# A norm by token halves, summed in PSUM and turned on TensorE, between an attention block and the last feed-forward layer

## What is computed

```
for i in range(DEPTH_2):                       # i = 1 is the last layer
    mix = ... moba_attention(h, b_w_qkv, b_w_out)   # ends in o @ w_out, 1024x1024
    h = layer_norm_2(DEEPNORM_ALPHA * h + mix, ln1_g[i], ln1_b[i])
    h = layer_norm_2(DEEPNORM_ALPHA * h + swiglu(h, f_w13[i], f_w2[i]), ln2_g[i], ln2_b[i])

def swiglu(x, w13, w2):
    g, u = jnp.split(x @ w13, 2, axis=-1)
    return (jax.nn.silu(g) * u) @ w2
```

## Time and profile before

| what | value |
|---|---|
| median of 3 runs | 1174.18 us |
| the profiled execution | 1169.08 us, its span 1167.3 us |
| PE busy, whole span | 1109.0 us, 95% |
| DVE, ACT busy | 807.5 us (69%), 614.9 us (53%) |
| mean granted TensorE clock | 0.986 |
| attention ends, output projection | about 924 to 957 us |
| norm x5 | 957 to 971 us |
| last feed-forward net | 971 to 1159 us |

### The profile page before, as it was taken

One profiled execution on the slowest core, in us unless ns is written; L12 is line 12 of the kernel. 1 busy time (PEld: TensorE's weight loads), 2 busy tenths in 40 slices (PEclk: granted clock), 3 DMA queues, 4 the chain that ended last, 5 costly groups with the idle time before them and its releaser, 6 DMA issues.

```text
span 1167.3 us, 20553 instructions
## 1 busy us (share of the span) xinstructions
PE 1109.0 (95%) x8544; PEld 1068.4 (92%) x8544; DVE 807.5 (69%) x1360; ACT 614.9 (53%) x1028; POOL 3.3 (0%) x13
## 2 busy tenths in 40 slices
PE   7998989999999998879989999999999999999997
PEld 7998878899999987679989999999999799999996
DVE  7988489877878787586666755555589656555555
ACT  5567444555555648742454554545455545545453
POOL 0000000000000000000000000000000000000000
PEclk9999999999999998989989999999999999999998
DMA  9985247257666523234224266565536332665620
GB/s 377 418 314 179 74 145 279 95 175 246 229 223 210 180 76 113 61 102 146 73 73 143 70 205 198 183 197 184 160 120 201 130 128 91 217 198 181 197 75 37
DMA packets 58557, 195.60 MB, mean 168 GB/s; under 512 B 10848, under 2 KB 11232, under 8 KB 58208
## 3 DMA queue, kind: packets, MB, share of 16 engines
q1 hardware_dynamic: 58464, 194.28, 49.1%
HBM read 192.94 MB, written 1.31 MB: 166 GB/s over the span
## 4 chain that ended last, share of the span: by engine, by line
PE 73%; DVE 17%; ACT 7%; issue 2%; SPq 1%; DMA 0%; POOL 0%; ACTq 0%; DVEq 0%; POOLq 0%
PE ps L512 61%; DVE lo L1475 4%; PE ps L725 3%; ACT hi L1008 2%; DVE raw L1462 2%; PE ps L610 2%; PE ps L519 2%; DVE B L1484 1%; PE ps L531 1%; DVE ev L1713 1%; DVE st L1492 1%; PE ps L507 1%; DVE ev L1710 1%; DVE B L1788 1%; DVE B L1497 1%
## 5 line engine op out<-in xcount | busy, mean ns | idle before, releaser
L512 PE MATMUL ps<-hh,hi 128*128 128x256 f32 x1792 | 511.2, 285 | 15.2 <-DVE hl L1509 3.5
L512 PE MATMUL ps<-hh,lo 128*128 128x256 f32 x1792 | 504.3, 281 | 0.0
L512 PE MATMUL ps<-hl,hi 128*128 128x256 f32 x1792 | 503.9, 281 | 0.0
L1475 DVE TENSOR_TENSOR lo<-raw,hi 128x1024 fp32r<-128x1024 f32 x311 | 378.2, 1222 | 171.9 <-ACT hi L1008 171.1
L512 PEld LDWEIGHTS ps<-hh,hi 128*128 128x128 f32 x1792 | 340.7, 190 | 19.9 <-issue 9.6
L1008 ACT ACTIVATE hi<-raw 128x1024 fp32r<-128x1024 f32 x311 | 324.2, 1051 | 51.9 <-PE ps L512 51.6
L512 PEld LDWEIGHTS ps<-hl,hi 128*128 128x128 f32 x1792 | 340.6, 190 | 1.1
L512 PEld LDWEIGHTS ps<-hh,lo 128*128 128x128 f32 x1792 | 340.7, 190 | 0.0
L512 PE MATMUL ps<-fh,hi 128*128 128x256 f32 x392 | 109.9, 280 | 3.9 <-ACT B L1112 2.9
L512 PE MATMUL ps<-fh,lo 128*128 128x256 f32 x392 | 108.8, 278 | 0.0
L512 PE MATMUL ps<-fl,hi 128*128 128x256 f32 x392 | 108.8, 277 | 0.0
(11 more groups left out here) (256 smaller groups left out, 1221.8 us busy)
## 6 DMA issues: line engine op xcount, KB each, us to landing
raw<-in_w SPq DMA_DIRECT2D x359, 512.0 KB, 4.2
B<-in_t SPq DMA_DIRECT2D x2, 512.0 KB, 4.8
xa<-in_x SPq DMA_DIRECT2D x1, 1024.0 KB, 10.4
B<-in_r SPq DMA_DIRECT2D x1, 1024.0 KB, 6.0
out<-h SPq DMA_DIRECT2D x4, 256.0 KB, 2.0
cst<-in_c SPq DMA_DIRECT2D x1, 864.0 KB, 8.3
B<-between SPq DMA_DIRECT2D x32, 4.0 KB, 1.6
vec<-in_v SPq DMA_DIRECT2D x1, 328.5 KB, 6.7
```

The costliest lines, as they stand in the source:

```text
L512: m = g.matmul(o, l, r, start=first and n == 0, stop=last and n == 2, skip_group_check=True)
L1475: g.tensor_tensor(lo[:, j % SPLIT, :], raw[:, PLACE[j] % RAW, :], hi[:, j % SPLIT, :].bitcast(F), ALU.subtract).then_inc(*up("lo", j))
```

## The change

It moves the residual and the norm between attention and the last net from channel-major to token-major, and takes the first four pairs of the last net in another cut.

- The old state (x4) is carried into banks 0 to 3 by `carry_in` before the projection; `bout` uses `rows_out_of`, so that the sum of residual and projection stands in PSUM by tokens: banks 0, 1 for tokens 0 to 127, banks 2, 3 for tokens 128 to 255. The last three units finish the first token half, then the second.
- `norm_tokens` takes statistics straight from PSUM, normalises a token half into `nt` (left 512 channels on DVE, right 512 on ACT), PE turns it (`turn_tok`, 8 transposes a half), and gain, bias and split follow in 128x128 pieces (`affine`, `high_part`, `low_part`; the right four channel chunks together in one 128x512 split). The residual add, both sums over channels and the 52 constant matmuls are gone.
- The weights of the first four pairs come as eight units `w13r1` by rows (128 channels x [512 gate | 512 up]) in place of eight tiles; `absorb` multiplies them into banks 0 to 3 by token halves: chunks 0 to 3 of the first half, with the second half's turn after the third, chunks 0 to 3 of the second half, then chunks 4 to 7 of both. Gate, product, eight transposes and one split on 128x512 per half give the four chunks for w2.

```diff
+def downs_at(j):
+    return {4: (0, 1), 5: (2, 3), FF - 1: ()}.get(j, (j - 2,))
...
+PARTS = ((0, 1), (1, 2), (2, 3), (3, 4), (4, 8))
...
-    w += swiglu(1)
+    w += [("w13r1", k) for k in range(8)]
+    for j in range(4, FF):
+        w += [("w131", j), ("w131", FF + j)] + [("w21", d) for d in downs_at(j)]
+    w += [("w21", FF - 3), ("w21", FF - 2), ("w21", FF - 1)]
...
+            def turn_tok(nid, c, frees):
+                for half in range(2):
+                    s.wait_ge(*at("norm_a" if half else "norm_v", (nid, c)))
+                    s.wait_ge(*frees[half])
+                    for i in range(4):
+                        k = 4 * half + i
+                        m = g.transpose(bank[4 + 2 * c + half][:, i * P:i * P + P], nt[:, c, k * P:k * P + P], ident)
+                    m.then_inc(*up("turned", (nid, c, half)))
+            def absorb(kind, nid, frees):
+                turn_tok(nid, 0, frees[0])
+                def unit(k, c):
+                    j = UNIT[kind, k]
+                    wh, wl = slot(j)
+                    v = slice(c * P, c * P + P)
+                    s.wait_ge(*at("lo", j))
+                    s.wait_ge(*at("hl", (nid, part_of(k), c)))
+                    for n in range(2):
+                        m = three(bank[2 * c + n][:, :], wh[:, n * 512:n * 512 + 512], wl[:, n * 512:n * 512 + 512],
+                                  hh[:, k, v], hl[:, k, v], k == 0, k == 7, flip=True)
+                    if c:
+                        m.then_inc(*up("unit", j))
+                for k in range(4):
+                    unit(k, 0)
+                    if k == 2:
+                        turn_tok(nid, 1, frees[1])
+                for k in range(4):
+                    unit(k, 1)
+                for k in range(4, 8):
+                    unit(k, 0)
+                    unit(k, 1)
+            def ffn_tokens(kup, kdown, kr, nid, frees):
+                def down(j, cs):
+                    rows_out_of(kdown, j, fh[:, j % 4, :], fl[:, j % 4, :], at("f4_lo", (kup, 1)) if j < 4 else at("f_lo", (kup, j)),
+                                cs, j == FF - 1)
+                absorb(kr, nid, frees)
+                for j in range(4, FF):
+                    for half in (0, 1):
+                        t = 2 * j + half
+                        tile(kup, j + half * FF, R3[t % 4], nid, at("ff_out", (kup, t - 4)) if t > 11 else
+                             at("f4_lo", (kup, t - 10)) if t > 9 else at("n_a" if half else "n_v", (nid, 7 if half else 3, 0)))
+                        if t == 8:
+                            for c in range(2):
+                                s.wait_ge(*at("f4", (kup, c)))
+                                s.wait_ge(*at("n_v", (nid, 3, 1)))
+                                s.wait_ge(*at("n_a", (nid, 7, 1)))
+                                for i in range(4):
+                                    m = g.transpose(bank[6 + c][:, i * P:i * P + P], half_ev[:, c, i * P:i * P + P], ident)
+                                m.then_inc(*up("f4_mm", (kup, c)))
+                    if j == 4:
+                        for k in range(8):
+                            carry_in(nid, k)
+                    for d in downs_at(j):
+                        down(d, (0, 1))
+                for c in range(2):
+                    for j in (FF - 3, FF - 2, FF - 1):
+                        down(j, (c,))
...
+            def bout(k, cs):
+                rows_out_of("bout", k, hh[:, k, :], hl[:, k, :], at("att_lo", k), cs, k == 7)
             turned(0)
             turned(1)
+            s.wait_ge(*at("v_a", 1))
+            s.wait_ge(*at("v_v", 3))
+            for k in range(4):
+                carry_in("x4", k)
             apply(0)
             turned(2)
+            for k in range(4, 8):
+                carry_in("x4", k)
             apply(1)
-            for k in range(8):
-                rows_in("bout", k, 0, hh[:, k, :], hl[:, k, :], at("att_lo", k), k == 0, k == 7,
-                        [at("v_a", 1), at("v_v", 3)] if k == 0 else [])
+            for k in range(5):
+                bout(k, (0, 1))
                 if k < 5:
                     turned(k + 3)
                 if k < 6:
                     apply(k + 2)
-            after("x5", lambda k: at("res", ("x5", k - k % 2)))
-            ffn("w131", "w21", "x5", at("hl", ("x5", 0)), tokens=True)
+            bout(5, (0,))
+            apply(7)
+            bout(6, (0,))
+            bout(7, (0,))
+            for k in range(5, 8):
+                bout(k, (1,))
+            ffn_tokens("w131", "w21", "w13r1", "x5", [[at(*a_free[4 + 2 * c + half]) for half in range(2)] for c in range(2)])
...
+            def norm_tokens(nid, gain, bias, j):
+                def deviation(c):
+                    s.wait_ge(*at("tmv", (nid, c)))
+                    g.activation(frs[:, c, :], fmv[:, c, 1:2], ACT.Sqrt, bias=eps[:, 0:1]).then_inc(*up("tsd", (nid, c)))
+                def normed(c):
+                    s.wait_ge(*at("tnm", (nid, c)))
+                    g.activation(nt[:, c, 512:1024], bank[2 * c + 1][:, :], ACT.Identity, scale=frs[:, c, :],
+                                 bias=fnm[:, c, :]).then_inc(*up("norm_a", (nid, c)))
+                def affine(c):
+                    s.wait_ge(*at("turned", (nid, c, 1)))
+                    for k in range(4, 8):
+                        i = (k - 4) * P
+                        g.activation(xa[:, k, c * P:c * P + P], bank[5 + 2 * c][:, i:i + P], ACT.Identity, scale=gain(k),
+                                     bias=bias(k)).then_inc(*up("n_a", (nid, k, c)))
+                def high_part(c, p):
+                    a, b = PARTS[p]
+                    s.wait_ge(*at("n_v" if a < 4 else "n_a", (nid, b - 1, c)))
+                    g.activation(hh[:, a:b, c * P:c * P + P], xa[:, a:b, c * P:c * P + P], ACT.Copy).then_inc(*up("hh", (nid, p, c)))
+                deviation(0)
+                high(j)
+                normed(0)
+                high(j + 1)
+                high_part(0, 0)
+                high_part(0, 1)
+                deviation(1)
+                high_part(0, 2)
+                normed(1)
+                high_part(0, 3)
+                affine(0)
+                for p in range(4):
+                    high_part(1, p)
+                high_part(0, 4)
+                affine(1)
+                high_part(1, 4)
...
+            def norm_tokens(nid, kind, gain, bias, j):
+                def stats(c):
+                    s.wait_ge(*(at("unit", UNIT[kind]) if c else at("tok", kind[0])))
+                    for n in range(2):
+                        g.bn_stats(fst[:, c, 6 * n:6 * n + 6], bank[2 * c + n][:, :]).then_inc(*up("tbn", (nid, c, n)))
+                    s.wait_ge(*at("tbn", (nid, c, 1)))
+                    g.bn_aggr(fmv[:, c, :], fst[:, c, :].rearrange("p (i n) -> p i n", i=2)).then_inc(*up("tmv", (nid, c)))
+                def normed(c):
+                    s.wait_ge(*at("tsd", (nid, c)))
+                    g.reciprocal(frs[:, c, :], frs[:, c, :]).then_inc(*up("trs", (nid, c)))
+                    s.wait_ge(*at("trs", (nid, c)))
+                    g.scalar_tensor_tensor(out=fnm[:, c, :], in0=fmv[:, c, 0:1], scalar=-1.0, in1=frs[:, c, :], op0=ALU.mult,
+                                           op1=ALU.mult).then_inc(*up("tnm", (nid, c)))
+                    g.tensor_scalar(nt[:, c, 0:512], bank[2 * c][:, :], fmv[:, c, 0:1], frs[:, c, :], ALU.subtract,
+                                    ALU.mult).then_inc(*up("norm_v", (nid, c)))
+                def affine(c, k):
+                    s.wait_ge(*at("turned", (nid, c, 0)))
+                    g.tensor_scalar(xa[:, k, c * P:c * P + P], bank[4 + 2 * c][:, k * P:k * P + P], gain(k), bias(k), ALU.mult,
+                                    ALU.add).then_inc(*up("n_v", (nid, k, c)))
+                def low_part(c, p):
+                    a, b = PARTS[p]
+                    v = slice(c * P, c * P + P)
+                    s.wait_ge(*at("hh", (nid, p, c)))
+                    g.tensor_tensor(hl[:, a:b, v], xa[:, a:b, v], hh[:, a:b, v].bitcast(F),
+                                    ALU.subtract).then_inc(*up("hl", (nid, p, c)))
+                stats(0)
+                normed(0)
+                low(j)
+                affine(0, 0)
+                affine(0, 1)
+                low_part(0, 0)
+                low_part(0, 1)
+                stats(1)
+                affine(0, 2)
+                low_part(0, 2)
+                normed(1)
+                affine(0, 3)
+                low(j + 1)
+                low_part(0, 3)
+                affine(1, 0)
+                affine(1, 1)
+                low_part(1, 0)
+                low_part(1, 1)
+                affine(1, 2)
+                affine(1, 3)
+                low_part(1, 2)
+                low_part(1, 3)
+                low_part(0, 4)
+                low_part(1, 4)
```

(42 more changed lines are left out.)

50 lines of the change are left out of this document (40 added, 10 removed).

## The result

| | median, us | runs | lowest to highest |
|---|---|---|---|
| before | 1172.61 | 15 | 1167.59 to 1174.87 |
| after | 1164.13 | 15 | 1160.44 to 1170.11 |

The ratio is 0.9933, with an interval of 0.9917 to 0.9949: faster, as forecast. Two later comparisons of the same two kernels gave 0.9961 [0.9946, 0.9976] and 0.9948 [0.9928, 0.9967], 5.2 and 7.1 us between the medians where this one has 8.5.

What follows compares the result with a forecast made beforehand. PE bounds the last net, so the 13.84 us hole ahead of it is the prize; less 3.1 carry, 1.65 turn and pause, 0.87 second turn, 0.87 pairs, 0.4 to 0.5 waits: gain 6.9 us, forecast 1167.3 us, range 1165.0 to 1171.5.

Steps and rivals of the forecast that it cites:

- The sum: Whole kernel: eight tiles' end moves from 993.4 to 986.5, gain 6.9 us; taken off 1174.18 this gives 1167.3.
- The carry of the old state: Sixteen products ahead of the projection cost 3.57 us, 0.43 covered, so the projection starts 3.14 us late.
- The projection by tokens: Attention's output projection: 12 matmuls of 512 columns per unit, 2.80 us; nothing won or lost, end at 960.20.
- The norm of the first half: Under the projection's last three units, 4.2 us: row ready before PE ends; without them 3.7 us would stand open.
- Turn and first unit: Between projection and last net: transposes 0.87 us, affine and splits, first matmul at 961.85; PE pauses 0.8 us.
- Eight units by token halves: Start of the last net: 96 matmuls 22.4 us, second turn 0.87, waits 0.5; all end at 985.6.
- What follows: Behind the eight units: four pairs' transposes add 0.87 us; gates and products are hidden, x5's carry stays 3.57.
- The fallen clock: Rival at the turn ahead of the last net: pause grows to about 2.9 us, time 1171.1; chance 0.07.
- The converters don't bind: Denies the rival that ACT and DVE bind the alternating halves: gain about 0, 1174; chance 0.06, half near 1170.
- the net gives nothing back: Denies the rival that weights bind the last net, earlier start becoming later wait: 1174.2, no change; chance 0.03.
- no low clock runs through the units: Denies the rival that all eight units run at 1.2 GHz: 22.4 us more, time 1191.8; chance 0.04.
- The rule against it: Removing 52 constant matmuls risks a clock fall after idle gaps; trace agreed for 3.15 us, not 2.69; new pause 0.8.

Runs made afterwards that it cites:

- fill_carry: Changed kernel plus 16 constant matmuls in PE's pause ahead of the carry of the old state: 1164.83 us, ratio 0.9937 to the kernel before.
- no_cover: Changed kernel with the projection's last three units done for both token halves at once: 1167.64 us, ratio 0.997 to the kernel before.
- tiles_first: Changed kernel with the last net's first four pairs again as tiles over all 256 tokens: 1172.29 us, ratio 1.002 to the kernel before.

## Why the prediction was right in the mechanism and wrong in the number

**The step that failed is "The sum"**, in its last part: "the same 6.9 off 1174.18 is 1167.3", with a range made of the bounds of the terms. The median of three runs stood 2.8 us above the mean of the 52 runs of before in the two later comparisons (1171.4), and 1.6 above the median of the 15 beside the result, of which these three are part. 1171.4 − 6.9 would have been 1164.5. Of the 3.2 us that were missing, 1174.18 − 1172.61 = 1.6 are this starting point. The other 1.6 are that the medians differ by 8.5 there and not by 6.9; the two later comparisons gave 5.2 and 7.1, and the mean of 33 runs of after is 1165.1, 6.3 below that of before. So a gain larger than the terms is not shown; the range left out that a median of a few runs moves by some us. The prediction had a sign of it in its own numbers: the profiled execution, at 1169.08, lies 5.1 below the median that it started from.

**The carry of the old state.** Mis-sized: I took the clock for safe because one execution stayed at 1.00 behind 2.69 us. It fell in all three traces of after, behind 2.27, for 1.65 us more: the projection's start is (939.94 − 929.97) − 5.43 = 4.54 us late. Where the clock stays, the 3.14 us are 2.89 (fill_carry).

**The projection by tokens.** A unit is 2.79 us, as said. By the timeline, projection to turn is 967.93 − 939.94 = 27.99 us, not 28.26: 0.3 better. "Nothing won or lost" overlooked that a unit of 24 matmuls takes 2.84 us in the chain of before, 0.05 more than one of 12:

```profile
936.67 2.84 PE ps L512 x24
```

Eight times 0.05 is 0.4, enough for the 0.3.

**The norm of the first half.** As argued: the row is ready at 967.4, PE done at 967.93. "Without them 3.7 us would stand open": no_cover lost 2.2. Its last unit, taken whole, still ends the first half's six matmuls 6 x 0.233 = 1.4 us before the second's, and 3.7 − 1.4 = 2.3.

**Turn and first unit.** 969.79 − 967.93 = 1.86 us, predicted 1.65; the pause 0.83, predicted 0.8. DVE's affine stands at 0.42 in the chain, where I took 0.30; the high part 0.32 and the low part 0.30 were near.

**Eight units by token halves.** From 969.79 to 996.40 it is 26.61 us with one tile of 2.83 in it: 23.78, where 22.4 + 0.87 + 0.5 = 23.77 was predicted. ACT's affine costs 1.48 / 4 = 0.37; I took 0.43. PE waits for none of these units' low parts for long: the longest row, 21.26 us for 102 matmuls, holds less than 0.3 of waiting.

**What follows.** From the carry of x5 to the end of the span it is 1168.3 − 1000.11 = 168.2 us after; before 1167.3 − 979.57 = 187.7, with seven tiles more behind it, of 2.8 each. The rest of the net is as long as it was.

With the measured terms, in order the fall, the rest of the carry, the projection and the turn, 6.9 − 1.65 + 0.25 + 0.3 − 0.2 = 5.6, and the two first traces differ by 5.6. With the clock alike in both kernels it is 6.9 (both with the fall) and 7.2 (neither, with fillers in after). So the terms of the change hold; what it gains in a given execution also hangs on where the clock falls.

**The rivals.** The fallen clock came, but in the changed kernel not where it was placed, and not because the norm's chain was too slow. At the turn it came in tiles_first, where PE waited 4.43 us. The condition that the rival set, a pause of about 2.9 us, does not hold: behind 2.27 and 2.70 us the clock fell too. The converters don't bind, the net gives nothing back, and no low clock runs through the units. That most of the gain hangs on the halves shows in tiles_first.

**The rule against it**, of the Trainium skill's "TensorE: Matmul & The Clock Gate", section "Why this matters for your kernels", speaks against idle gaps between bursts of matmuls, and means longer ones than the 2.27 us here. The traces agree for the 4.43 us of tiles_first. At the carry the clock fell behind 2.27 us all the same, for 1.65 us, in three traces of after, and not in that of no_cover, with the same gap. So neither my one row nor the rule settles a gap of this length.

## What to carry to other kernels

A hole ahead of a bound engine is worth its length less what takes its place, and the terms can be had to a few tenths from rows of the same form; but take the time they are subtracted from, and the range, from the spread of many executions, not from three. Here a norm split into halves paid because its consumer could start on half of it; without that nothing was left, some 2 us by the estimate at full clock. Then look at what the moved work now waits for: here copies placed a few instructions too late cost about half as much as the whole change gains.

## What the runs showed of the hardware

- The granted clock behind a short pause is not settled by its length: ahead of the carry, 2.27 us idle was followed by about half clock in four traces (three of after, one of tiles_first) and by 1.00 in that of no_cover; in the kernel before, 2.69 us kept 1.00 and 2.70 us fell to 0.50. Behind 4.43 us, at the turn of tiles_first, it fell to 0.50 as well.
- A run's time goes with its mean granted clock: over the 140 runs of the seven kernels timed here, each kernel about its own mean, 0.01 of clock more goes with some 5.6 us less. This is a relation between the runs; what sets the clock of an execution was not found.
